# Turned probabilities of a run copied together through two banks, gate steps ahead of them, and a branch tile cast by ScalarE, in a two-layer streaming encoder trunk

## What is computed

```python
def hybrid_layer(x, ...):
    h = rms_norm(x, g_mix)
    qa, ka, va, qb, kb, vb, gate_logits = split(h @ w_in)
    y_a = chunk_band_relbias_attention(qa, ka, va, rel_table) @ w_branch_a   # 8 heads, band of 9 chunks of 64
    y_b = sliding_window_sink_gqa(rope(qb), rope(kb), vb, sinks) @ w_branch_b  # 8 heads, 2 kv heads, sinks
    g_a, g_b = split(sigmoid(gate_logits + b_gate))
    x = x + (g_a * y_a + g_b * y_b) @ w_out
    h2 = rms_norm(x, g_ffn)
    g_part, u_part = split(h2 @ w_gate_up)
    return x + (silu(g_part) * u_part) @ w_down
# softmax of A: p = softmax(q k^T * scale + bias);  of B: p = exp(s - m) / (sum + exp(sink - m))
# two layers, then a last rms_norm
```

## Time and profile before

| | before |
| --- | --- |
| runs | 2642.32, 2646.60, 2647.32 us |
| profiled execution, its own time | 2642.42 us |
| its span | 2640.6 us |
| TensorE busy | 2589.2 us, 98% |
| VectorE busy | 1820.5 us, 69% |
| ScalarE busy | 1054.0 us, 40% |
| POOL busy | 288.4 us, 11% |
| attention stage, layer 0 and 1 | 272.96 to 508.13 and 1576.47 to 1811.65 us |

### The profile page before, as it was taken

How to read it: one execution, slowest core, us unless ns; L and a number is a source line. 1 busy time by engine, 2 the same in 40 slices (tenths; PEclk the granted TensorE clock), 3 DMA queues, 4 the chain that set the end, 5 groups by cost and what they waited for, 6 DMA issues and landing times. The chain is left out here.

```text
span 2640.6 us, 35934 instructions
## 1 busy us (share of the span) xinstructions
PE 2589.2 (98%) x12824; PEld 2092.7 (79%) x12824; DVE 1820.5 (69%) x3319; ACT 1054.0 (40%) x2133; POOL 288.4 (11%) x450
## 2 busy tenths in 40 slices
PE   8999999999999999999999999999999999999998
PEld 6888776788888888888788886677888888888886
DVE  8766455544787778768996664555448878786687
ACT  6222366532533333344542224664225333333444
POOL 0000222344000000000000011224440000000000
PEclk9999999999999999999999999999999999999999
DMA  4323443253132332385423244423521332234843
GB/s 155 122 104 129 152 129 110 100 196 129 40 133 87 104 116 104 103 274 167 151 104 120 104 153 133 131 88 132 176 112 64 112 116 100 88 112 149 266 121 127
DMA packets 201519, 337.49 MB, mean 128 GB/s; under 512 B 18816, under 2 KB 81152, under 8 KB 201344
## 3 DMA queue, kind: packets, MB, share of 16 engines
q1 hardware_dynamic: 193120, 312.00, 35.8%
q10 hardware_dynamic: 8224, 23.20, 2.6%
HBM read 241.28 MB, written 92.93 MB: 127 GB/s over the span
## 5 line engine op out<-in xcount | busy, mean ns | idle before, releaser
L1386 PE MATMUL ps<-op_hi,up_hi 128*128 128x512 f32 x1232 | 479.9, 390 | 2.5 <-DVE third_sum L2916 2.5
L1388 PE MATMUL ps<-op_hi,up_lo 128*128 128x512 f32 x1232 | 479.3, 389 | 0.0
L1387 PE MATMUL ps<-op_lo,up_hi 128*128 128x512 f32 x1232 | 479.3, 389 | 0.0
L1386 PE MATMUL ps<-in_hi,up_hi 128*128 128x512 f32 x728 | 285.0, 392 | 2.1 <-DVE up_lo L2421 2.1
L1388 PE MATMUL ps<-in_hi,up_lo 128*128 128x512 f32 x728 | 283.8, 390 | 0.0
L1387 PE MATMUL ps<-in_lo,up_hi 128*128 128x512 f32 x728 | 283.8, 390 | 0.0
L1386 PEld LDWEIGHTS ps<-op_hi,up_hi 128*128 128x128 f32 x1232 | 231.2, 188 | 51.0 <-issue 3.3
L1388 PEld LDWEIGHTS ps<-op_hi,up_lo 128*128 128x128 f32 x1232 | 231.2, 188 | 48.1
L1387 PEld LDWEIGHTS ps<-op_lo,up_hi 128*128 128x128 f32 x1232 | 231.3, 188 | 48.0
L2021 ACT ACTIVATE up_hi<-up_raw 128x512 fp32r<-128x512 f32 x252 | 158.1, 630 | 278.2 <-PE ps L1388 271.2
L1386 PE MATMUL ps<-act_hi,dn_hi 128*128 128x512 f32 x616 | 240.3, 390 | 1.1 <-DVE dn_lo L3091 1.1
(11 more groups left out here) (249 smaller groups left out, 4911.0 us busy)
## 6 DMA issues: line engine op xcount, KB each, us to landing
up_raw<-w_gu SPq DMA_DIRECT2D x42, 1024.0 KB, 5.1
act_raw<-ff_saved SPq DMA_DIRECT2D x154, 256.0 KB, 2.7
w_quarter<-w_lin SPq DMA_DIRECT2D x52, 512.0 KB, 4.5
w_raw<-w_lin SPq DMA_DIRECT2D x48, 512.0 KB, 3.8
ff_saved<-ff_block SPq DMA_DIRECT2D x88, 256.0 KB, 2.0
ff_saved<-ff_mix SPq DMA_DIRECT2D x66, 256.0 KB, 2.0
gated<-gates_saved SPq DMA_DIRECT2D x32, 512.0 KB, 4.1
dn<-w_dn_a SPq DMA_DIRECT2D x48, 256.0 KB, 4.0
```

What stands on the lines that cost most here:

```text
L1386: pe.matmul(out, w1, x1, start=first, stop=False, skip_group_check=True)
L1387: pe.matmul(out, w1, x0, start=False, stop=False, skip_group_check=True)
L1388: return pe.matmul(out, w0, x1, start=False, stop=last, skip_group_check=True)
```

## The change

- The probabilities of a run are turned together (`turn_run`): in A each unit has a bank of its own (5 and 1), in B the four blocks of a run share bank 5. The fifth blocks of a wide pair go side by side in bank 7. `take_turned` copies a B run in one piece of 512 columns and the two fifth blocks in one; there is one pair of buffers `probs_t`. On ScalarE the copies of the run before now come behind `soften` of the first unit of the new run.
- All gate steps of a run stand together, behind `weigh` and ahead of the turning, in bank 0 alone (half 1 in bank 1). A new half waits until the one before it is scaled. `last_gates` gives its first two steps to the end of the stage.
- Pairs of B are weighed in the second run after their own; the values are transposed at other places; `invert` of A comes one unit later.
- The high part of the first branch tile is cast by ScalarE in one instruction of 128x1024 (`raise_branch`), and POOL makes the low part before the last scalings, not after them.

Of the three functions `attention` in it, the first is TensorE's, the second ScalarE's, the third POOL's.

```diff
-CONV_START = (1, 3, 6, 9, 10, 13, 17, 20) + tuple(
-    g * UNITS_PER_GROUP + r for g in range(1, GROUPS) for r in (20 - UNITS_PER_GROUP, 24 - UNITS_PER_GROUP, 4, 9))
+CONV_START = (1, 3, 6, 4, 10, 8, 20, 20) + tuple(
+    g * UNITS_PER_GROUP + r for g in range(1, GROUPS) for r in (24 - UNITS_PER_GROUP, 28 - UNITS_PER_GROUP, 4, 9))
...
-FILL_A = ((3, 3, 3, 3, 2, 3, 1, 2, 1, 1, 0, 1, 1, 1, 0, 1), (1, 1, 0, 1, 0, 1, 0, 1, 0, 1, 0, 1, 0, 1, 0, 0))
-FILL_B = (14, 14, 14, 12)
+FILL_A = ((8, 4, 4, 2, 2, 2, 2, 0),) + ((2, 2, 2, 1, 1, 1, 1, 0),) * (GROUPS - 1)
+FILL_B = ((4, 4, 3, 3),) * (GROUPS - 1) + ((2, 2, 2, 2),)
...
 def weighed_at(u):
-    s = u + 3
-    return s + (2 if s % UNITS_PER_GROUP >= PHASE and s % 4 == 2 else 0)
+    return run_end(run_end(u) + 1) + 1
...
+def gates_scaled_at(i):
+    return max(0, run_end(FILL_END[i]))
...
-        t_ps = bank(5)
-        last_ps = bank(7)[:, 2 * P:3 * P]
+        t_ps = (bank(5), bank(1))
+        last_ps = bank(7)[:, 2 * P:4 * P]
...
             def attention(L):
                 ...
                 for s in range(UNITS + 3):
+                    starts = s <= UNITS and s == run_start(s)
+                    if s < UNITS and starts:
                         scores(L, s)
                     for u in weighed_in(s):
                         weigh(L, u)
-                    for i, k in steps[:1]:
+                    for i, k in fill_steps(s):
                         gate_step(L, i, k)
-                    u = s - 2
-                    if 0 <= u < UNITS:
-                        if unit(u)[0] == "A":
-                            turn(L, u)
-                        elif u % 2:
-                            turn(L, u - 1)
-                            turn(L, u)
+                    if s > 0 and starts:
+                        turn_run(L, s - 1)
                     for eight in inverses_at(s, 0):
                         turn_inverse(L, eight)
-                    for i, k in steps[1:]:
-                        gate_step(L, i, k)
...
             def attention(L):
                 ...
-                    if 2 <= s < UNITS + 2 and (unit(s - 2)[0] == "A" or s % 2 == 1):
-                        take_turned(L, s - 2)
                     if s < UNITS:
                         soften(L, s)
+                    if s > 0 and s == run_start(s):
+                        take_turned(L, s - 1)
+                    if s == run_start(s):
+                        for c, part in turns_at(s):
+                            take_values(L, c, part)
                     if eight_at(s, EIGHT) is not None and unit(s - 1)[0] == "B":
                         soften_sinks(L, eight_at(s, EIGHT))
...
+            def raise_branch(L):
+                act.wait_ge(tile_loaded[raw], ...)
+                act.wait_ge(tile_used, L * TILES + GATE_TILES)
+                act.activation(w_hi[slot][:, :, :], w_raw[raw][:, :, :], ACT.Copy).then_inc(o_hi_ready, 1)
...
             def attention(L):
+                    if s == UNITS + 2:
+                        split(L, GATE_TILES)
                     for quarter in quarters_at(s, SCALED_AFTER):
                         if quarter < POOL_QUARTERS:
                             scale_heads(L, quarter)
-                split(L, GATE_TILES)
```

More of the change, by code:

```diff
@@ L201, in load_at @@
     other = last_in_place(c)
-    free = 0 if other is None else max(0, CONV_START[other] + CONV_SPAN[of_kind(other)] + 1)
+    free = 0 if other is None else max(0, second_turn(other) + 1)
     rank_of_user = SWAP_USERS.index(c) if c in SWAP_USERS else 0
@@ L305, in turned_through @@
 def turned_through(u):
-    return sum(2 if wide(v) else 1 for v in range(u + 1))
+    runs = {run_start(v): 1 if unit(v)[0] == "B" else 3 if wide(v) else 2 for v in range(u + 1)}
+    return sum(runs.values())
 def scores_through(u):
     return u + 1 + sum(wide(v) for v in range(0, u + 1, 2))
-def groups_turned(u):
-    return sum(2 if wide(v) else 1 for v in range(u + 1) if unit(v)[0] == "A" or v % 2)
 def last_wide(u):
     return max((v for v in range(u + 1) if wide(v)), default=None)
[L321 to L332, removed]
 HEAD_PAIRS = UNITS // 2
@@ L670, in turned_to @@
         def turned_to(u):
-            return probs_t[turned_place(u)]
+            return probs_t[:, u % 2, :] if unit(u)[0] == "A" else probs_t[:, 0, u % 4 * P:(u % 4 + 1) * P]
         def odd_values(block):
@@ L1556, in weigh @@
                     blocks = [vb[:, chunk // 2, :] if chunk % 2 or chunk == 0 else odd_values(chunk // 2 - 1)]
-                    turns = [turned_to(u)[:, e * P:(e + 1) * P] for e in range(2)]
+                    turns = [turned_to(u - 1), turned_to(u)]
                     if p == 0:
@@ L1921, in attention, with take_turned @@
-            def attention(L):
-                for s in range(UNITS + 2):
-                    for c, part in turns_at(s - 1):
-                        take_values(L, c, part)
-                    if 2 <= s < UNITS + 2 and (unit(s - 2)[0] == "A" or s % 2 == 1):
-                        take_turned(L, s - 2)
+            def take_turned(L, last):
+                mixer, _, _, p = unit(last)
+                first = run_start(last)
+                made = L * TURNS + (turned_through(first - 1) if first > 0 else 0)
+                taken = L * HEAD_PAIRS + weighed_through(last + 1)
+                if mixer == "B":
+                    act.wait_ge(turned, made + 1)
+                    act.wait_ge(head_done, taken)
+                    act.activation(probs_t[:, 0, 0:HALF], t_ps[0][:, :], ACT.Copy).then_inc(turned_ready, 1)
+                    return
+                cols = min(key_blocks(mixer, p) * P, HALF)
+                for e in range(2):
+                    act.wait_ge(turned, made + e + 1)
+                    if e == 0 and taken > 0:
+                        act.wait_ge(head_done, taken)
+                    act.activation(probs_t[:, e, 0:cols], t_ps[e][:, 0:cols], ACT.Copy).then_inc(turned_ready, 1)
+                if wide(last):
+                    act.wait_ge(turned, made + 3)
+                    act.activation(probs_t[:, :, HALF:A_COLS], last_ps.rearrange("p (e n) -> p e n", e=2),
+                                   ACT.Copy).then_inc(turned_ready, 1)
@@ L2786, in attention @@
                         if eight is not None:
-                            sunken = unit(EIGHT * eight)[0] == "B"
-                            if late == 0 and sunken:
+                            if late == 0 and unit(EIGHT * eight)[0] == "B":
                                 add_sinks(L, eight)
-                            if late == (1 if sunken else 0):
+                            if late == 1:
                                 invert(L, eight)
```

174 lines of the change are left out of this document (95 added, 79 removed).

## The result

| | before | after |
| --- | --- | --- |
| median | 2646.9 us | 2676.3 us |
| profiled execution, its span | 2642.4, 2640.6 | 2674.8, 2673.0 |
| attention stage by starts, layer 0 and 1 | 235.2, 235.2 | 254.2, 251.2 |
| from the stage to the first branch projection | 3.1, 4.1 | 0.2, 0.2 |
| branch projections by starts | 88.5, 88.3 | 89.5, 89.8 |

The change makes the kernel slower: after/before is 1.0112, 95% interval 1.0093 to 1.0131. 2661 was predicted, with a range up to 2674; the direction was right and the loss twice as large as said.

What follows compares the result with a forecast made beforehand. TensorE, busy 98% of the span, was taken as the bound; 2642.4 - 31.6 + 0.7 + 53.0 - 10.0 + 5.5 = 2660.0, stated as 2661 us for the median. Own range 2650 to 2672, wider range 2627 to 2674.

Steps and rivals of the forecast that it cites:

- waits removed and regrouping: Attention stage: all 15.8 us of waits per layer go, -31.6; gate steps gathered behind weighing cost +0.7.
- new waits at the boundaries: Between runs, scores wait for the last row maximum with no gate steps between: 26.5 us per layer, +53.0.
- end of the stage and branch projections: After attention: the wait for POOL and two half-clock stretches go, -10.0; late scalings delay the first branch half, +5.5.
- first B run: Its boundary: units wait for A's last turned blocks to leave the buffers, 0.80 late; 3.0 us per layer.
- second: Second B run's boundary: maxima stand behind the copy of the inverses, 1.23 late, 2.0 in group 0; 5.7 per layer.
- third: Third B run's boundary: inverses wait for the sinks' exponential behind ScalarE's copy, 1.8 to 1.97 late; 7.4 per layer.
- fourth: Fourth B run's boundary: maxima wait behind copied inverses and two heads, 1.03 late three times; 3.1 per layer.
- first A run: After B, groups 1 to 3: late maxima, then a late scaling of the gate half; 4.8 us per layer.
- fourth A run: Its boundary in mixer A: 0.3 late behind rotary work, 0.9 us per layer.
- tail: End of the stage: pairs weighed straight behind their turning wait for the copy, 1.6 us per layer.
- slower still, by the clock: Rival: idling about 2 us at eight third-run boundaries drops the clock to 0.50 each time, 13 us, 2673; chance 0.05.
- the late o_lo: First branch half: VectorE makes the last four o_lo late, after POOL's delayed scalings; +2.75 us per layer.

Runs made afterwards that it cites:

- e2: Kernel after, with VectorE's copies of turned inverses and heads in mixer B moved behind the run's fourth row maximum; 2661.8 us, ratio 1.0058.
- e3: As e2, and VectorE also makes the inverses of B's first eight units behind the third run's fourth maximum; 2650.3 us, ratio 1.0018.
- the kernel at 2606.9: Kernel after, with TensorE's gate steps moved behind the turning, inverses and values, right ahead of the next scores; ratio to before 0.9851.
- after_again: The kernel after, unchanged, run and profiled once more; 2676.9 us, ratio 1.0119.
- e5_low_behind: Kernel after, with POOL's low part of the first branch tile put back behind the last two scalings; 2670.5 us, ratio 1.0089.
- e4_clock_filler: Kernel after, with 14 transposes that make nothing ahead of the scores at the ten boundaries with the longest waits; 2674.6 us.
- e4_filler_in_both: Kernel after, with 8 and 6 unused transposes in a boundary's two idle stretches, 13 in the last group's single one; 2671.7 us, ratio 1.0096.

## Why the prediction was wrong

The forecast was +17.6 us from profile to profile; it was +32.4. By its own steps:

| step | forecast | measured |
| --- | --- | --- |
| waits removed and regrouping, pieces of the two stages | -31.6 + 0.7 | -31.6 + 2.6 |
| new waits at the boundaries | 53.0 | 54.0 |
| stretches at half clock inside the stages | 0 | 9.3 |
| end of the stage and branch projections | -10.0 + 5.5 | -4.3 together |
| the rest | 0 | 2.4 |

(The last row is 0.8 of waits under 0.1 each and 1.6 outside: the stage starts 0.85 later, at 273.81, 0.5 of it in the wait for the first x_sb, and 0.75 I have not followed.)

- **The boundaries held.** Forecast and measured per layer, layer 0 and 1: first B run 3.0, measured 4.2 and 3.9; second 5.7, 5.5 and 5.7; third 7.4, 7.8 and 7.6; fourth 3.1, 2.8 and 2.8; first A run 4.8, 4.7 and 5.0; fourth A run 0.9, 0.3 and 0.4; tail 1.6, 1.7 and 1.6. The sinks' exponential stood at 395.05, 0.8 behind the turned blocks' end. The first B run was dearer, as the first values of group 0 wait 0.96 for the copy of the fifth blocks.
- **One reason behind them was incomplete.** The sum priced one chain at each boundary, VectorE's. At the third and fourth a second one, over the values' halves, ran beside it and ended within 0.2 us of it at the fourth. The size came out right, in part by luck, since the two ended together; what an edit would bring did not, as e2 and e3 showed.
- **The step that failed is the clock.** The sum has no term for it inside the stages, and six spells cost 9.3 us there, of the 14.8 by which the forecast was short; without them the profiled execution would have read 2665.5, inside the range. (Of the other 5.5, the regrouping is 1.9, the boundaries 1.0, the end 0.2 and the rest 2.4.) The rival "slower still, by the clock" said 2673 and had a chance of 0.05; it is in the main what happened, at 2676. It counted eight third-run boundaries, of which four had a drop, and left out the second run of group 0, where the wait of 1.95 was in the same sum and two of two had one. The chance came from one row, the stretch from 39 to 41 us at 1.00. That row is one draw: of the 14 profiles of this study six have a drop there, 41.4 to 43.9 us from the start. A single profile can't exclude that a gap of 2 us costs a drop.
- **The end held.** The wait for POOL went, no drop stands behind the stage (those at 510.4 and 1828.0 lie inside it), and the first projections lost 2.6 and 3.0 us where 2.75 was said. The size is partly luck: the late o_lo, which were to be all of it, cost 1.8, and 0.76 and 1.04 were the load of the next tile behind the late rows in SyncE's list, which the working did not have.
- **Regrouping** cost 1.3 us per layer and not 0.35, small in any case. The prediction looked for a gain of 4 us behind weighing; there is one on the other side: with gate steps behind the turning, the pieces take 217.8 us for 220.9.
- **Joined copies.** The Trainium skill, Perfetto Trace Analysis, Optimizing Scalar/DVE Operations, says that breaking up instructions may let work be done sooner where ScalarE holds up other engines. By that the joining would be a loss. No run here splits the copies, so its price is not shown; the kernel at 2606.9 has all of them joined.

## What to carry to other kernels

Where an engine's list ends a step with work that others must answer, put filler between that work and the next thing that needs the answer; gathering the filler ahead of it turned the answers into waits here, at every boundary of the B runs. Here the same gate steps in the one place and in the other are 70 us apart. Count all chains that end at a boundary before pricing an edit that shortens one of them. And where a forecast makes TensorE idle for about 2 us at many places, price a spell at half clock at a good part of them: of the ten boundaries with 1.8 to 2.3 us of idle time, six, three and five had one in the three profiles of kernels that have them all (after, `after_again`, `e5_low_behind`).

## What the runs showed of the hardware

A spell at 1.2 GHz cost 1.55 us wherever the stage lengths let it be read (9.3 us for six, 3.1 for two), and it came in some executions of a kernel and not in others after the same idle stretch: near 42 us in 6 of 14 profiles, and behind a wait of 2.3 us early in layer 1 (1317 to 1355, by the kernel) in 5 of the 14. Inside the stages it followed waits of 1.8 to 2.3 us with two exceptions (1725.5 in `after_again` and 354.5 in `e4_clock_filler`, both behind a 0.9 and a 0.6 to 0.7). The kernel of the second has no wait over 1.3 in its stages; of the nine other profiles of which that is true, none had a drop there. Filling the idle time with transposes that make nothing kept the drops away in the one profile of `e4_filler_in_both`.
